# Tokens loaded first, queries as three fp32r products, and the first decode pair's cache transposes inside the last head pair

## The reference, cut to what matters

```python
z = x @ w_in                                   # 1024 -> 384 + 256 + 32
cq = rms_norm(z[..., :Q_LORA], q_norm)
ckv = rms_norm(z[..., Q_LORA:Q_LORA + KV_LORA], kv_norm)
kr = rope(z[..., Q_LORA + KV_LORA:], pos)
q = (cq @ w_q_up).reshape(B, L, N_HEADS, QK_NOPE + QK_ROPE)   # 16 heads, 64 + 32
q_rope = rope(q[..., QK_NOPE:], pos)
q_lat = jnp.einsum('blhn,chn->blhc', q[..., :QK_NOPE], w_uk)
...
s = (q_lat . c_kv + q_rope . k_rope) * ATTN_SCALE    # causal mask, softmax
o = p . c_kv, then w_uv and w_o
```

## Time and profile before

| | before |
|---|---|
| median of 3 runs | 1406.89 us (1406.12 to 1407.55) |
| the profiled execution | 1406.64 us, its span 1404.8 us |
| PE busy | 1379.1 us (98%), 10379 instructions |
| DVE busy | 639.1 us (45%) |
| ACT busy | 516.6 us (37%) |
| POOL busy | 232.3 us (17%) |
| transfers | 111.14 MB, mean 79 GB/s |

### The profile page before, as it was taken

One profiled execution on the slowest core, in us unless ns is written; L12 is line 12 of the kernel. 1 busy time (PEld: TensorE's weight loads), 2 busy tenths in 40 slices (PEclk: granted clock), 3 DMA queues, 4 the chain that ended last, 5 costly groups with the idle time before them and its releaser, 6 DMA issues.

```text
span 1404.8 us, 26582 instructions
## 1 busy us (share of the span) xinstructions
PE 1379.1 (98%) x10379; PEld 1283.5 (91%) x10379; DVE 639.1 (45%) x929; ACT 516.6 (37%) x832; POOL 232.3 (17%) x318
## 2 busy tenths in 40 slices
PE   9989999899999999999999999999999999999997
PEld 9847777557999999999999999999999999999996
DVE  3546666433572332223333678877522322333335
ACT  3236565423352221122221468854422211222234
POOL 0030010000551000000001525565600000000043
PEclk9999999999999999999999999999999999999999
DMA  8231110122233332232232222322333322322301
GB/s 220 65 91 28 24 28 19 60 87 94 61 90 91 90 105 90 60 90 80 75 119 76 68 68 69 92 78 74 95 90 101 103 81 60 89 77 85 123 1 64
DMA packets 180836, 111.14 MB, mean 79 GB/s; under 512 B 25896, under 2 KB 179069, under 8 KB 180768
## 3 DMA queue, kind: packets, MB, share of 16 engines
q1 hardware_dynamic: 180176, 109.41, 26.8%
q0 software_dynamic: 592, 0.79, 0.2%
HBM read 107.15 MB, written 3.02 MB: 78 GB/s over the span
## 4 chain that ended last, share of the span: by engine, by line
PE 91%; DVE 3%; ACT 2%; issue 1%; SPq 1%; POOL 0%; DMA 0%; DVEq 0%; ACTq 0%; POOLq 0%
PE ps L533 55%; PE ps L562 8%; PE ps L625 4%; PE ps L809 3%; PE ps L822 3%; PE ps L1165 2%; PE ps L845 1%; PE ps L1113 1%; PE ps L800 1%; PE ps L704 1%; PE ps L1000 1%; PE ps L955 1%; PE ps L1022 1%; PE ps L697 1%; PE ps L963 1%
## 5 line engine op out<-in xcount | busy, mean ns | idle before, releaser
L533 PE MATMUL ps<-xh,wl 128*128 128x280 f32 x1472 | 310.5, 292 | 0.0
L533 PE MATMUL ps<-xh,wh 128*128 128x280 f32 x1472 | 308.8, 291 | 0.7 <-ACT sg L1493 0.7
L533 PE MATMUL ps<-xl,wh 128*128 128x280 f32 x1472 | 307.9, 290 | 0.0
L1234 ACT ACTIVATE wh<-raw 128x2048 fp32r<-128x2048 f32 (+2 forms) x79 | 162.9, 2063 | 204.1 <-PE ps L533 179.3
L1583 DVE TENSOR_TENSOR wl<-raw,wh 128x2048 fp32r<-128x2048 f32 (+2 forms) x79 | 197.9, 2505 | 87.7 <-ACT wh L1234 87.6
L533 PEld LDWEIGHTS ps<-xh,wh 128*128 128x128 f32 x1472 | 233.9, 188 | 1.3 <-ACT sg L1493 1.1
L533 PEld LDWEIGHTS ps<-xh,wl 128*128 128x128 f32 x1472 | 234.6, 189 | 0.0
L533 PEld LDWEIGHTS ps<-xl,wh 128*128 128x128 f32 x1472 | 232.2, 188 | 0.0
L1920 DVE TENSOR_TENSOR ht<-sg,ps 128x560 f32<-128x560 f32 x44 | 32.5, 738 | 269.0 <-PE ps L533 264.8
L2111 POOL TENSOR_TENSOR acc<-xT 128x560 f32<-128x560 f32 x4 | 7.7, 1933 | 750.6 <-DVE xT L1806 648.5
L1495 ACT ACTIVATE hh<-ht 128x560 f32 (+1 forms) x44 | 29.6, 672 | 262.1 <-DVE ht L1920 262.1
(11 more groups left out here) (349 smaller groups left out, 2491.8 us busy)
## 6 DMA issues: line engine op xcount, KB each, us to landing
raw<-in_ffn_w_gu SPq DMA_DIRECT2D x176, 256.0 KB, 3.7
raw<-in_ffn_w_down SPq DMA_DIRECT2D x48, 384.0 KB, 4.3
raw<-in_lru_w_in SPq DMA_DIRECT2D x16, 512.0 KB, 4.5
Ctok<-in_cache_latent SPq DMA_DIRECT2D x48, 128.0 KB, 2.1
raw<-in_mla_w_o SPq DMA_DIRECT2D x16, 256.0 KB, 3.6
raw<-in_ffn_w_down SPq DMA_DIRECT2D x16, 256.0 KB, 5.0
raw<-in_lru_w_o SPq DMA_DIRECT2D x16, 256.0 KB, 3.3
wq<-in_mla_w_q_up SPq DMA_DIRECT2D x16, 144.0 KB, 2.4
```

The lines of the kernel that those rows point to most:

```text
L533: mm = pe.matmul(ps[:, 1024 * jp + 512 * h:1024 * jp + 512 * h + TH], w[:, k, col:col + P], x[:, k, h * TH:(h + 1) * TH], start=(k == 0 an ...
L1234: act.activation(wh[u][:, 0:w], raw[u][:, 0:w], ACT.Copy).then_inc(hi_ok, 1)
```

## The change

- **Tokens first.** The identity and the tokens are issued ahead of the first weights, and these come as two pieces of two k-tiles and four of one, with semaphores of their own (`y_out`, `pg_in[5]`, `raw_in[0]`). ACT and DVE split the pieces behind token tiles 3 and 4 (`first_weights`). `warm(38)` becomes `warm(14)` and the wide ones go. `first_part` runs k 0 and 1 of both tiles, then 2 and 3, then the rest.
- **Three-product queries.** Queries take z and the weights apart (`zqh`, `zql`, `wqh`, `wql`) and use three fp32r products for each fp32 one. ACT and DVE split z during the V stage (kt == 2), POOL splits each head's weights in `swap`. POOL's loop over the heads is written out, and the first two swaps go ahead of four of the six row outputs.
- **Orders.** Keys of the first pair go ahead of its queries; in odd heads `turn(p, 0, 1)` moves up behind `scores(p, 1, 4)` and `keys(p + 1)` ahead of `turn(p, 0, 3)`.
- **The first decode pair.** Its `fill` steps 0 to 9 move into the last head and the turns behind it, in banks 0 and 7 (those of queries and keys); the second sample's turned cache has a place of its own (`CT1a`). For this the last head's `read_pt(p, 0, 3)` goes ahead of its last exponential.

```diff
+            first = raw[0][:, 0:W_D].rearrange("p (k n) -> p k n", k=KD)
+            for k0, done in ((0, y_out), (2, pg_in[5])):
+                sp.dma_start(first[:, k0:k0 + 2, :], win[:, k0:k0 + 2, QL_R:QL_R + KV_R]).then_inc(done, 16)
+            for k in range(4, KD):
+                sp.dma_start(first[:, k, :], win[:, k, QL_R:QL_R + KV_R]).then_inc(raw_in[0], 16)
...
-            warm(38)
-            warm_wide(5, 512)
-            warm_wide(4, 280)
-            warm_wide(4, 256)
+            warm(14)
             pe.wait_ge(in_id, 16)
-            for t in range(4):
+            for t in range(5):
                 turn_x(t)
                 warm(4)
+            pe.wait_ge(s_xl0, 9)
+            for jp in range(2):
+                first_part(jp, 0, (0, 1))
+            pe.wait_ge(s_xl0, 12)
+            for jp in range(2):
+                first_part(jp, 0, (2, 3))
             pe.wait_ge(lo_ok, 1)
-            pe.wait_ge(s_xl0, 6)
-            first_part(0, 0, lambda k: turn_x(4) if k == 1 else None)
-            first_part(1, 0)
-            pe.wait_ge(s_xl0, 10)
+            for jp in range(2):
+                first_part(jp, 0, range(4, KD))
...
                 for k in range(KQ):
-                    mm = pe.matmul(ps[:, 512 * n:512 * n + TH], wq[u][:, k, :], z[:, k, n * TH:(n + 1) * TH],
-                                   start=(k == 0), stop=(k == KQ - 1))
+                    for i, (w, x) in enumerate(((wqh, zqh[k][:]), (wqh, zql[:, k, :]), (wql, zqh[k][:]))):
+                        mm = pe.matmul(ps[:, 512 * n:512 * n + TH], w[u][:, k, :], x[:, n * TH:(n + 1) * TH],
+                                       start=(k == 0 and i == 0), stop=(k == KQ - 1 and i == 2))
...
+                    if i == 4:
+                        if last:
+                            fill(0, 0)
+                            fill(0, 1)
+                        else:
+                            queries(h + 1, v, 0)
...
+                else:
+                    fill(0, 2)
+                    fill(0, 3)
...
-            for i in range(4):
+            for i in range(2):
                 turn(HEADS // 2 - 1, 1, i)
...
+            turn(HEADS // 2 - 1, 1, 2)
+            fill(0, 4)
+            fill(0, 5)
+            turn(HEADS // 2 - 1, 1, 3)
+            for i in range(6, 10):
+                fill(0, i)
             outputs(HEADS // 2 - 1, 1)
...
+                pool.wait_ge(wq_sw, h * 4 + 2)
+                pool.tensor_copy(wqh[u][:], wq[u][:]).then_inc(wq_sw, 1)
+                pool.wait_ge(wq_sw, h * 4 + 3)
+                pool.tensor_tensor(wql[u][:], wq[u][:], wqh[u][:].bitcast(F32), ALU.subtract).then_inc(wq_sw, 1)
```

More of the change, by code:

```diff
@@ L887, in head @@
                     scores(p, u, i)
-                    if u == 1:
-                        turn(p, *((0, 0), (0, 1), (0, 2), (1, 4), (0, 3))[n])
-                    elif not first:
+                    if i == 3 and u == 1 and not last:
+                        keys(p + 1)
+                    if i == 4:
+                        turn(p, 0, 0)
+                        turn(p, 0, 1)
+                    elif u == 1 and i > 0:
+                        turn(p, *((0, 2), (1, 4), (0, 3))[i - 1])
+                    elif u == 0 and not first:
                         turn(p - 1, 1, i)
@@ L895, in head @@
                         mm.then_inc(wt_sum, 1)
-                    if i == 4 and not last:
-                        queries(h + 1, v, 0)
+                    if i == 4:
+                        if last:
[3 more added lines that the diff above has]
+                            queries(h + 1, v, 0)
                     if i == 2 and u == 1:
@@ L905, in head @@
                         queries(h + 1, v, 0)
-                    if i == 3 and u == 1 and not last:
-                        keys(p + 1)
                 if not last:
@@ L923, in _ @@
             pe.wait_ge(s_vd, 5)
-            keys(0)
             pe.wait_ge(s_kp2, 2)
@@ L1024, in w_o_part @@
                 return mm
-            for i in range(10):
-                fill(0, i)
             pe.wait_ge(ql_rd, HEADS // 2)
@@ L1241, in split_next, with first_weights @@
                     split(c + 1, q + u, 1 - u, w)
-            split(0, 0, 0, W_D)
+            def first_weights(piece):
+                act.wait_ge((y_out, pg_in[5], raw_in[0])[piece], (16, 16, 64)[piece])
+                at = slice(512 * piece, 512 * piece + 512 if piece < 2 else W_D)
+                act.activation(wh[0][:, at], raw[0][:, at], ACT.Copy).then_inc(s_xh0 if piece < 2 else hi_ok, 1)
             for t in range(5):
@@ L1284, in _ @@
                     root(1)
+                if kt == 2:
+                    for k in range(KQ):
+                        act.wait_ge(s_z, KC + k + 1)
+                        act.activation(zqh[k][:], z[:, k, :], ACT.Copy).then_inc(s_zroot, 1)
                 for t in ROWS_AT[kt]:
@@ L1363, in _ @@
             head(HEADS // 2 - 1, 1)
-            for i in range(4):
+            for i in range(3):
                 read_pt(HEADS // 2 - 1, 1, i)
+            fills(0, (2,))
+            read_pt(HEADS // 2 - 1, 1, 3)
             act.wait_ge(d_q, 1)
@@ L2070, in _ @@
                 pool.wait_ge(wq_in[u], 16)
-                swap(u)
+                swap(u, u)
+            for t in range(2, 6):
+                rows_out(t)
             pool.wait_ge(s_ve, 5)
```

206 lines of the change are left out of this document (125 added, 81 removed).

## The result

| | median, us | range | runs |
|---|---|---|---|
| before | 1406.51 | 1405.65 to 1407.55 | 4 |
| changed | 1392.67 | 1391.33 to 1396.58 | 4 |

The ratio is 0.9906 [0.9891, 0.9921], 13.2 us less. A second comparison in five rounds (first experiment) gave 0.9893 [0.9879, 0.9907], 15.0 us less. I had forecast 1386, so the gain was 13 to 15 us instead of 20.8. The median of 1392.67 lies at the upper end of the range of 1380.5 to 1393, and outside the forecast's own range of 1382 to 1389.5.

The account below looks back on a forecast made before the run. TensorE, busy 98% of the span, was taken to bound the kernel. Terms -6.6 -1.7 -7.1 -5.4 = -20.8 took 1406.64 to 1385.8, 1386 us on the median; range 1380.5 to 1393, the forecast's own 1382 to 1389.5 (58%).

Parts of the forecast that it names:

- part 1: Start of the kernel: tokens loaded before weights, first part ends at 28.2 instead of 34.8 us; -6.6, bounds -3.6 and -8.
- part 3: The 16 heads: three fp32r products per fp32 query product, plus reordering; -7.1 us, bounds -3 and -9.3.
- Moving keys ahead of the last transpose reorders work of one engine and costs nothing: Odd heads: the moved keys were put at no cost, since K's copies start earlier.
- The second half gives 0.31: Odd heads: the second half of the queries saves 0.31 us, 7 times: 2.2 us.
- rival (a): Heads: exponential and maximum, not TensorE, end every wait; heads give 2 to 3 us, total about 1390; 14%.
- So 0.62 us a head: Heads: six fp32 query products take 2.92 us, six fp32r triples 2.30, saving 0.62 us per head.
- (c): Heads: POOL is late, the port costs 0.5 us for each of 14 swaps, +7, total 1393; 6%.
- (d): Heads: POOL's new work blocks DVE between scores and exponential, 14 x 1.7 = 24 us, total 1410; 3%.
- Part 2: Start of the heads: keys ahead of queries, first scores near 91.3 instead of 93.29; -1.7 us, bounds 0 and -2.4.
- Rival (b): Start: TensorE's rate stays low in the first products or tokens land later; part 1 gains 1 us, total 1391.5; 13%.
- Part 4: Last head: first decode pair's transposes fill its holes, decode scores at 264.3 instead of 269.73; -5.4 us, bounds -6.6 and -3.
- rival (e): Last head: moved transposes push ACT's exponentials and lengthen it equally; Part 4 gives 1 us, total 1390; 6%.

Follow-up runs that it names:

- after_again: The first experiment: the changed kernel once more, no edit, in five rounds; 1391.52 us, ratio 0.9893 to the kernel before.
- fp32_queries: Changed kernel with queries as one fp32 product again and no splits of z and weights, orders kept; ratio 0.9923, 4.5 us slower than after_again.
- turn_back: k_read_first with `turn(p, 0, 1)` and ScalarE's copy of it between the odd head's first two scores, as before the change; ratio 0.9870.
- keys_back: Changed kernel with the next pair's keys and the copies of K behind the last transposes, as in the kernel before; ratio 0.9895.
- k_read_first: keys_back with DVE's copy of K ahead of the last normalising; 1388.83 us, ratio 0.9869, 2.7 us faster than after_again.
- best1: k_read_first with POOL's second swap and split of query weights behind the four last row outputs; 1388.28 us, ratio 0.9863.
- pool_more: Changed kernel with one more 128x384 subtraction on POOL for each of the 16 query-weight splits; ratio 0.9912, 3.5 us slower than after_again.

## Why the prediction was wrong

Stage by stage, forecast and measured (after_again against before, part 1 against the mean of the profiles):

| part | forecast | measured |
|---|---|---|
| 1, tokens first | -6.6 | -5.3 |
| 2, start of the heads | -1.7 | -1.3 |
| 3, three-product queries and orders | -7.1 | -3.1 |
| 4, fills in the holes | -5.4 | -4.9 |
| sum | -20.8 | -14.6 |

**The step that failed is part 3**, by 4.0 us. Of these 2.6 lie in the odd heads, mostly by the keys moved ahead of the last transpose, which I put at nothing and which cost 0.37 us a pair; 0.7 in seven even heads, which give 0.52 us instead of 0.62; and 0.7 in the first even head, which gives nothing. Three of its sentences failed, and one thing is missing from it.

"Moving keys ahead of the last transpose reorders work of one engine and costs nothing" is wrong. Keys need the outputs' bank, which DVE reads at `L1787` to 140.74 in the timeline of after_again. Keys start 1.45 us after the fourth block's scores in both orders; before, the transposes stood in that time, and now TensorE waits 0.32 there and does the transposes behind. fp32_queries prices the orders at 0.37 a pair, six times; that it is the keys and not the transposes of `turn(p, 0, 1)` follows from turn_back, where the place of these was worth nothing. I had looked at what the keys feed and not at what they need.

"The second half gives 0.31" in the odd head holds only if nothing else ends that stretch. In the order of before the outputs also wait for DVE's copy of K (it ended at 152.85, the outputs started at 153.16), which was just hidden by six fp32 records. With three products and that order (keys_back) the odd head takes 12.37 us, before 12.36: nothing of the saving arrives. It arrives where K's copy is early: 0.26 in the changed orders (12.73 to 12.47) and 0.25 in those of k_read_first (12.28 to 12.03). So something else than TensorE does end the odd head's wait, but not what rival (a) named: it is DVE's reads and copies of other banks, not exponential or maximum. In the even head rival (a) was wrong. In the changed kernel the odd head is 0.11 longer than before (12.36 + 0.37 - 0.26).

"So 0.62 us a head" was a size. The products follow each other every 0.128 us as in part 1, but 2.92 us for the fp32 block reached to the start of the outputs, which come 0.33 us behind the last record where records are 0.236 apart. The fp32r block has the same extra at its end (135.40 to 135.61, 0.21 instead of 0.13), which 2.30 left out. The even head gives 0.52 (8.57 to 8.05) instead of 0.62. The price of 0.08 us for each switch between fp32 and fp32r, in the text ahead of fp32_queries, is not shown by this: where fp32 follows fp32 the extra at the end is as large.

What it lacks is the first even head, which I counted with the others. It gives nothing (7.4 us to the first 16 rows before, 7.5 changed): the wait of 1.7 us there, explained under rivals (c) and (d), takes it back.

**Part 1** was right in mechanism. Its size was off mainly because both kernels scatter with the moment at which the fillers' rate steps up. 28 filler records took 4.75 to 6.24 us, and eleven profiles with 14 fillers have V start at 55.6 to 57.1 (mean 56.4); before, 62.3 and 61.1. My sum started from the late one, and it put the end of the 28 records at 6.4 us, where 0.214 us for each from 1.44 on give 7.4. The tiles' pace of 1.68 us came out right. Two engines share it: TensorE's transposes and fillers (0.77 and 0.91) have no gap between them, and neither have DVE's two subtractions and copy (0.62, 0.53 and 0.53 us on the chain of after_again). I had only the first; which of the two would hold the tiles without the other, no run shows.

**Part 2** gave 1.3 us where the clock stayed up. That the rows would be ready about when the keys end was nearly right: in after_again queries start 2.19 us after the keys, 0.06 us behind ScalarE's copy of the last rows; in best1, with earlier rows, 1.69 us after. These 0.5 us are about what is missing. Rival (b), a low clock in the first products, did not come: the rate had stepped up before them in every profile. The fall that did come stood at the end of the V stage of one profile and cost 1.7 us.

**Part 4** was right within 0.5 us, though 1.4 of its 4.9 us come without the fills in the holes. The pages of samples 4 and 5 were not waited for; a later wait for cached latents (0.6 us near 288 in after_again) stood in the kernel before as well (0.7). All behind moved as one block, and rival (e) is out. What I had not counted is the clock: it fell in two of the three profiles that have the holes of the last head as before (3.6 and 3.8 us).

**Rivals (c) and (d), POOL's port.** No wait of queries for POOL appeared in the heads. But DVE's normalising gets longer, in groups of DVE by form (busy us, mean ns; the first is of the kernel before, the others of the changed one):

```profile
L1689 DVE TENSOR_SCALAR Pr<-Pr,rsum 128x512 f32<-128x512 f32 x16 | 7.8, 486 | 0.6
```

```profile
L1765 DVE TENSOR_SCALAR Pr<-Pr,rsum 128x512 f32<-128x512 f32 x16 | 10.3, 646 | 0.6
L1757 DVE TENSOR_REDUCE mx<-ps 128x1 f32<-128x512 f32 x16 | 11.0, 688 | 0.7 <-PE ps L844 0.5
```

The normalising went from 486 to 646 ns in the mean, the maximum stayed at 688 (687 before). Seven of the sixteen are long, 682 to 1228 ns in after_again, one in each pair, while POOL subtracts; with fp32_queries, which leaves the splits out, the longest is 493. The Trainium skill, "SBUF — State Buffer", "Who interferes with whom", says that a reduction never contends and that tensor_scalar may; the trace agrees.

In the first head this cost time, once. In after_again a normalising of 1.23 us beside POOL's subtraction makes DVE's copy of Q late, and the last 16 rows wait for it:

```profile
90.71 1.01 POOL L2150 TENSOR_TENSOR wql<-wq,wqh 128x384 fp32r<-128x384 f32 x1
90.77 1.23 DVE L1765 TENSOR_SCALAR Pr<-Pr,rsum 128x512 f32<-128x512 f32 x1
92.03 0.74 DVE L1776 TENSOR_TENSOR Q<-ps,trig 64x560 f32<-64x560 f32 x1
93.02 1.04 PE L847 MATMUL ps<-K,Q 128*16 128x512 f32 x4 [1.65 <-DVE Q L1776]
```

In turn_back POOL's subtraction starts 0.22 us after that normalising. The normalising keeps its 0.48 us, the subtraction takes 1.12 instead of 1.01, and the wait is 0.6 us shorter:

```profile
91.57 0.48 DVE L1763 TENSOR_SCALAR Pr<-Pr,rsum 128x512 f32<-128x512 f32 x1
91.79 1.12 POOL L2148 TENSOR_TENSOR wql<-wq,wqh 128x384 fp32r<-128x384 f32 x1
93.20 1.04 PE L847 MATMUL ps<-K,Q 128*16 128x512 f32 x4 [1.03 <-ACT Qs L1376]
```

pool_more, where that normalising takes 0.49 us as well, has the same 6.9 us to the first 16 rows. This is rival (c)'s mechanism with one swap instead of fourteen. In the later pairs the stretch is off the chain: in pool_more these normalisings take at most 537 ns instead of 682 to 994, and the heads are as long.

## What to carry to other kernels

A saving on the busiest engine counts only in those stretches in which that engine ends the next wait; read each stretch for which engine is second, and by how little (here a wait of 0.3 us for DVE's copy swallowed the 0.26 us that the products give). When an operation is moved ahead, ask what it needs as well as what it feeds: here a bank that another engine was still reading. And when two profiles are compared, cut them at the same events and look at the granted clock of each cut first; one fall costs as much as a part of the change.

## What the runs showed that I had not expected

- A fall of the clock is not bound to the program alone: a stall of 1.7 us near 917 was followed by a fall to 0.60 in one execution of the changed kernel and by none in another (near 912), nor in the kernel before (927 to 930). The falls held the lower level for 3 to 4 us (those at 79 and 919) or for 10 (those in the last head), and cost 1.7 to 3.8 us each.
- The first fillers run at two rates: their records are 0.214 us apart at first and 0.111 later, with the step after 13 to 27 records, in kernels that are the same up to there. The granted clock reads 1.00 in both stretches. The step alone moves the whole kernel by 1.5 us from one execution to the next.
- A normalising of DVE that started 0.06 us behind POOL's subtraction took 1.23 us instead of 0.48; one that started 0.22 us ahead of it kept its 0.48. The long one delayed TensorE by 0.6 us only where DVE's next result was waited for.
